# A hybrid encoder block with mixture of experts: bias products in two halves, SSD state products and output moved, router in column groups

## The reference

```
xn = rmsnorm(h); proj = xn @ w_in                  # q,k,v,r, z, xbc, dt, gates
o  = gla_scan(forward) + gla_scan(backward)        # gated linear attention, 4 heads
xbc = silu(dwconv(xbc)); xs, bm, cm = split(xbc)
y  = ssd_scan(forward) + ssd_scan(backward) + ssd_d * xs   # 4 groups of 8 heads of 64
y  = rmsnorm_per_group(y * silu(z))
mix = sigmoid(g_gla) * (o @ w_up_gla) + sigmoid(g_ssd) * (y @ w_up_ssd)
h  = h + mix @ w_out
logits = rmsnorm(h) @ w_router + b_router          # 32 experts, the best 4 per token
for each expert: hdn = x @ w1 + b1; act = gate * sigmoid(1.702 * gate) * (lin + 1); y = act @ w2 + b2
h  = h + sum(gates * y);  out = rmsnorm(h)
```

## Time and profile before

| | |
|---|---|
| runs | 2020.31, 2022.59, 2026.1 us, median 2022.59 us |
| the profiled execution | 2024.75 us |
| its span | 2023.0 us, 26649 instructions |
| busy share of the span | PE 97%, PEld 79%, DVE 77%, ACT 60%, POOL 12% |
| granted TensorE clock, mean | 0.987 |
| DMA | 540.21 MB, mean 267 GB/s |

### The profile page before, as it was taken

How to read it: one execution, slowest core, us unless ns; L and a number is a source line. 1 busy time by engine, 2 the same in 40 slices (tenths; PEclk the granted TensorE clock), 3 DMA queues, 4 the chain that set the end, 5 groups by cost and what they waited for, 6 DMA issues and landing times.

```text
span 2023.0 us, 26649 instructions
## 1 busy us (share of the span) xinstructions
PE 1969.2 (97%) x9610; PEld 1597.8 (79%) x9610; DVE 1555.2 (77%) x1499; ACT 1219.2 (60%) x1064; POOL 246.9 (12%) x175
## 2 busy tenths in 40 slices
PE   8999999999999999999999999999999999999998
PEld 6787777777768788778888888888888888888886
DVE  6655447878864335579889898998989899898987
ACT  6545444635434223357777777777777777777775
POOL 0000204263421000101010100001000001101000
PEclk9999999999999999789999999999999999999999
DMA  5233444354426934489999999999999999999995
GB/s 148 53 96 88 148 118 137 94 175 153 130 64 238 295 100 161 148 303 385 373 372 381 368 379 367 375 377 366 383 366 375 369 375 378 366 377 372 370 361 195
DMA packets 211720, 540.21 MB, mean 267 GB/s; under 512 B 16339, under 2 KB 131445, under 8 KB 174728
## 3 DMA queue, kind: packets, MB, share of 16 engines
q1 hardware_dynamic: 204368, 518.46, 70.2%
q0 software_dynamic: 7056, 20.80, 4.5%
q10 hardware_dynamic: 232, 0.08, 0.0%
HBM read 512.08 MB, written 31.20 MB: 269 GB/s over the span
## 4 chain that ended last, share of the span: by engine, by line
PE 65%; DMA 3%; issue 2%; DVE 1%; SPq 1%; ACT 1%; POOL 0%; DVEq 0%; POOLq 0%; ACTq 0%
PE ps L1847 32%; PE ps L1907 16%; PE ps L244 3%; PE ps L245 3%; PE ps L246 3%; DMA residual_rows<-late_b 2%; PE ps L1840 1%; PE ps L1815 1%; PE ps L1880 1%; SPq L2276 1%; DMA ssd_low<-ssd_out_T 1%; PE ps L1636 1%; PE ps L2010 1%; PE ps L1556 1%; DVE w_low L1745 0%
## 5 line engine op out<-in xcount | busy, mean ns | idle before, releaser
L1745 DVE TENSOR_TENSOR w_low<-ring_b,w_high 128x2048 fp32r<-128x2048 f32 x192 | 437.5, 2288 | 51.1 <-ACT w_high L1739 49.1
L1745 DVE TENSOR_TENSOR w_low<-ring_a,w_high 128x2048 fp32r<-128x2048 f32 x192 | 437.1, 2287 | 49.8 <-ACT w_high L1739 47.8
L1739 ACT ACTIVATE w_high<-ring_a 128x2048 fp32r<-128x2048 f32 x192 | 368.4, 1920 | 153.8 <-PE ps L1847 117.1
L1739 ACT ACTIVATE w_high<-ring_b 128x2048 fp32r<-128x2048 f32 x192 | 368.7, 1921 | 145.6 <-PE ps L1847 108.9
L1847 PE MATMUL ps<-w_high,rows_high 128*128 128x512 f32 x1024 | 403.4, 394 | 0.6 <-DVE w_low L1745 0.4
L1847 PE MATMUL ps<-w_high,rows_low 128*128 128x512 f32 x1024 | 400.3, 391 | 0.0
L1847 PE MATMUL ps<-w_low,rows_high 128*128 128x512 f32 x1024 | 399.7, 390 | 0.0
L1847 PEld LDWEIGHTS ps<-w_high,rows_high 128*128 128x128 f32 x1024 | 193.1, 189 | 42.7 <-DVE w_low L1745 3.0
L1847 PEld LDWEIGHTS ps<-w_high,rows_low 128*128 128x128 f32 x1024 | 192.8, 188 | 41.2
L1847 PEld LDWEIGHTS ps<-w_low,rows_high 128*128 128x128 f32 x1024 | 193.0, 189 | 39.9
L239 DVE TENSOR_TENSOR unit_low<-unit_raw,unit_high 128x1024 fp32r<-128x1024 f32 x108 | 142.6, 1330 | 98.5 <-ACT unit_high L234 98.4
(11 more groups left out here) (381 smaller groups left out, 2882.7 us busy)
## 6 DMA issues: line engine op xcount, KB each, us to landing
ring_a<-in_w SPq DMA_DIRECT2D x192, 1024.0 KB, 7.7
ring_b<-in_w SPq DMA_DIRECT2D x192, 1024.0 KB, 7.5
unit_raw<-in_w_in SPq DMA_DIRECT2D x80, 512.0 KB, 4.0
temps<-cum_rows SPq DMA_DIRECT2D x16, 1024.0 KB, 8.3
unit_raw<-in_w_up_ssd SPq DMA_DIRECT2D x16, 512.0 KB, 7.9
ssd_out_T<-y_high SPq DMA_DIRECT2D x4, 1024.0 KB, 6.3
ssd_out_T<-y_low SPq DMA_DIRECT2D x4, 1024.0 KB, 6.5
ssd_high<-ssd_out_T SPq DMA_DIRECT2D x4, 1024.0 KB, 11.4
```

The lines of the kernel that those rows point to most:

```text
L1739: nc.scalar.activation(w_hi[:, split_at(it, j)], slot(at, 1)[:, 0, :], ACT.Copy).then_inc(w_hi_ok, 1)
L1745: nc.vector.tensor_tensor(w_lo[:, split_at(it, j)], slot(at, 1)[:, 0, :], w_hi[:, split_at(it, j)].bitcast(F32), ALU.subtract).then_inc(w_ ...
```

## The change

- `ssd_pe`: the two state products of step 0 come after tile 1's products inside the chunk, ahead of the fifth piece, where they came after tile 3's. In `ssd_dve`, `to_end(0)`, which feeds them, comes ahead of `masked(0)`, where it came after the split of the fifth piece.
- `ssd_act`: the third piece's copy and the first two `keep_x` come ahead of `silu(4)`.
- The last group's output isn't stored and loaded: the mix reads `y_hi` and `y_lo` where they are. They get the place that `ssd_high3` had, and `in_w` moves behind `x_e`.
- The router: each matmul with 128 stationary columns becomes four with 32, each in its column group.
- The bias: `b1_s` is half as wide; partitions 0 to 63 hold the gate half (high, low), 64 to 127 the linear half plus one. Each of the four matmuls reads one half of the partitions. b1 comes in four loads; the cleared rows and the row of ones go.
- The end adjusts a semaphore's count (`r_in_at`), since group 3's is no longer raised by loads.

```diff
@@ SSD, TensorE
+            def states_pe(s):
+                for d in range(2):
+                    t = step_tiles(s)[d]
+                    pe.wait_ge(xe_ok, g * 6 + 2 * s + d + 1)
+                    if s == 0 and g:
+                        pe.wait_ge(ss_ok, g * 6)
+                    nc.tensor.matmul(ps[:, 6 + d, :], b_n[:, t, :], (x_e if s else in_w)[d], start=True, stop=True).then_inc(su_ps, 1)
...
                 last.then_inc(yi_ps, 1)
+                if t == 1:
+                    states_pe(0)
                 if 0 < t < 3:
                     piece(pe, n0 + 3 + t)
...
-                    if s < NT - 1:
-                        pe.wait_ge(xe_ok, g * 6 + 2 * s + d + 1)
...
+                if 0 < s < NT - 1:
+                    states_pe(s)
                 piece(pe, n0 + 6 + s)
@@ SSD, ScalarE
             silu(3)
+            piece_take(act, n0 + 2)
+            keep_x(0)
+            keep_x(1)
             silu(4)
-            piece_take(act, n0 + 2)
-            for i in range(4):
-                keep_x(i)
+            keep_x(2)
+            keep_x(3)
             silu(5)
@@ SSD, VectorE
             v.wait_ge(cb_ps, g + 1)
+            to_end(0)
             masked(0)
...
             split_low(v, n0 + 4)
-            to_end(0)
             y_begin(0)
@@ last group's output
-                store_y(sp, g)
+                if g < GR - 1:
+                    store_y(sp, g)
...
-            sp.wait_ge(y_out, 32 * GR)
+            sp.wait_ge(y_out, 32 * (GR - 1))
+            sp.wait_ge(y_lo_ok, GR * 4)
...
-            load_y(3)
@@ router
-                last = nc.tensor.matmul(ps[:, 2 * t, 0:NE], f_T[:, k, tokens(t)], wr_w[:, k, :], start=k == 0, stop=k == NK - 1)
+                for u in range(4):
+                    rows = slice(u * 32, (u + 1) * 32)
+                    last = nc.tensor.matmul(ps[rows, 2 * t, 0:NE], f_T[:, k, t * P + u * 32:t * P + (u + 1) * 32], wr_w[:, k, :],
+                                            start=k == 0, stop=k == NK - 1, tile_position=(0, u * 32))
@@ bias
-            for n in range(4):
-                nc.tensor.matmul(ps[:, n, :], pick[:, :], b1_s[:, n * 512:(n + 1) * 512], start=True, stop=False)
+            for n in range(2):
+                for half in range(2):
+                    rows = slice(half * 2 * NE, (half + 1) * 2 * NE)
+                    nc.tensor.matmul(ps[:, 2 * half + n, :], pick[rows, :], b1_s[rows, n * 512:(n + 1) * 512], start=True, stop=False)
...
-            for half in range(2):
-                sp.dma_start(b1_rows[half * NE:(half + 1) * NE, :], b1).then_inc(b1_in, 16)
+            for part in range(4):
+                cols = slice(part // 2 * DFF, (part // 2 + 1) * DFF)
+                sp.dma_start(b1_rows[part * NE:(part + 1) * NE, :], b1[:, cols]).then_inc(b1_in, 16)
...
                     nc.scalar.activation(b1_s[0:2 * NE, :], b1_rows[0:2 * NE, :], ACT.Copy).then_inc(b1_hi, 1)
+                    nc.scalar.activation(b1_s[2 * NE:P, :], b1_rows[2 * NE:P, :], ACT.Identity, bias=1.0).then_inc(b1_hi, 1)
...
-            nc.vector.memset(b1_s[2 * NE:P, :].bitcast(F32), 0.0).then_inc(one_zero, 1)
...
+                    nc.vector.scalar_tensor_tensor(b1_s[linear_low, :], b1_rows[linear_low, :], 1.0, b1_s[linear_low, :].bitcast(F32),
+                                                   ALU.add, ALU.subtract).then_inc(b1_lo, 1)
...
-            nc.vector.tensor_tensor(expert_at, ident[:, 0:NE], ident[:, NE:2 * NE], ALU.add).then_inc(one_zero, 1)
-            v.wait_ge(one_zero, 2)
-            nc.vector.memset(expert_at[2 * NE:2 * NE + 1, :], 1.0).then_inc(b1_lo, 1)
+            nc.vector.tensor_reduce(expert_at, ident[:].rearrange("p (k e) -> p e k", e=NE), AX.X, ALU.add).then_inc(b1_lo, 1)
```

More of the change, by code:

```diff
@@ L1038, in build @@
         s_st = [take(GW) for _ in range(2)]
-        in_w = [take(GW) for _ in range(2)]
         cb_d = take(SEQ).rearrange("p (t i) -> p t i", t=NT)
@@ L1045, in build @@
         z_odd = take(NT * GW).rearrange("p (t n) -> p t n", t=NT)
+        used[0] = AT_Y - AT_T + (GR - 1) * 2 * NT * GW
         y_hi = at("y_high", AT_T + used[0], NT * GW, F32R)
@@ L1053, in build @@
         x_D = x_e
+        in_w = [take(GW) for _ in range(2)]
         def by_head(ap):
@@ L1123, in ssd_pe @@
                         nc.tensor.matmul(ps[:, 2 + d, :], xcT[:, 5, tokens(t)], s_st[d], start=True, stop=True).then_inc(in_ps, 1)
-                    if s < NT - 1:
-                        pe.wait_ge(xe_ok, g * 6 + 2 * s + d + 1)
-                        if s == 0 and g:
-                            pe.wait_ge(ss_ok, g * 6)
-                        nc.tensor.matmul(ps[:, 6 + d, :], b_n[:, t, :], (x_e if s else in_w)[d], start=True, stop=True).then_inc(su_ps, 1)
+                if 0 < s < NT - 1:
+                    states_pe(s)
                 piece(pe, n0 + 6 + s)
@@ L1494, in build @@
         oT_hi, oT_lo = (at(n, AT_XN + i * NK * SEQ, NK * SEQ, F32R) for i, n in enumerate(("gla_high", "gla_low")))
-        yT_s = [[at(f"ssd_{n}{g}", AT_Y + g * 4096 + i * 2048, 4 * SEQ, F32R) for i, n in enumerate(("high", "low"))] for g in range(GR)]
+        yT_s = [[at(f"ssd_{n}{g}", AT_Y + g * 4096 + i * 2048, 4 * SEQ, F32R) for i, n in enumerate(("high", "low"))] for g in range(GR - 1)] + [[y_hi, y_lo]]
         mixT_hi, mixT_lo = (at(n, AT_MIX + i * NK * SEQ, NK * SEQ, F32R) for i, n in enumerate(("mix_high", "mix_low")))
@@ L1508, in build @@
         ring = [at(n, o, RING // 2 * UNIT) for n, o in (("ring_a", AT_GATES), ("ring_b", AT_RAW))]
-        b2_w, b1_rows = misc[:, 0:D], late_c[:, D:D + 2 * DFF]
+        b2_w, b1_rows = misc[:, 0:D], late_c[:, D:D + DFF]
         def slot(s, k):
@@ L1565, in build @@
         b1_lo = sem("b1_lo")
-        one_zero = sem("one_zero")
         slot_ok = sem("slot_ok")
@@ L1580, in build @@
         a_hi, a_lo = (small_r(n, NK * WIDE) for n in ("act_high", "act_low"))
-        b1_s = small_r("bias_split", 2 * DFF)
+        b1_s = small_r("bias_split", DFF)
         pick = small_r("pick", WIDE)
@@ L1981, in build @@
         r_in = y_in
+        r_in_at = (48, 48, 48, 16)
         sT_ps, sT_ps0 = small_ps, 1
@@ L2088, in residual @@
             def residual(t):
-                pe.wait_ge(r_in[t], 48)
+                pe.wait_ge(r_in[t], r_in_at[t])
                 for j in range(2):
@@ L2140, in finish_dve @@
                     v.wait_ge(fin_ps, fin_ps0 + t + 1)
-                    v.wait_ge(r_in[t], 48)
+                    v.wait_ge(r_in[t], r_in_at[t])
                     row = fin[:, t, :].rearrange("p (a b) -> p a b", a=2)
@@ L2330, in mix_tensor @@
                         if c == 0 and k % 4 == 0:
-                            pe.wait_ge(y_in[q // 4], 32)
+                            if q // 4 < GR - 1:
+                                pe.wait_ge(y_in[q // 4], 32)
+                            else:
+                                pe.wait_ge(y_lo_ok, GR * 4)
                         y = tuple(chunk(a, q % 4) for a in yT_s[q // 4])
@@ L2485, in mix_vector @@
                 if t == 1:
[L2486 to L2488 removed]
+                    v.wait_ge(b1_hi, 2)
+                    gate_low, linear_low = slice(NE, 2 * NE), slice(3 * NE, 4 * NE)
+                    nc.vector.tensor_tensor(b1_s[gate_low, :], b1_rows[gate_low, :], b1_s[gate_low, :].bitcast(F32),
                                             ALU.subtract).then_inc(b1_lo, 1)
+                    nc.vector.scalar_tensor_tensor(b1_s[linear_low, :], b1_rows[linear_low, :], 1.0, b1_s[linear_low, :].bitcast(F32),
+                                                   ALU.add, ALU.subtract).then_inc(b1_lo, 1)
             def pick_rows(t):
```

7 lines of the change are left out of this document (1 added, 6 removed).

## The result

| | before | after |
|---|---|---|
| median of five runs | 2020.31 us (2019.21 to 2026.10) | 2009.46 us (2007.44 to 2010.57) |
| ratio of the times | | 0.994, 95% interval 0.9923 to 0.9957 |
| the profiled execution | 2024.75 us | 2009.46 us |
| its span, mean granted clock | 2023.0 us, 0.987 | 2007.7 us, 0.989 |
| instructions | 26649 | 27027 |

What follows compares the result with a forecast made beforehand. TensorE's own instructions were taken to bound the expert loop, DMA loaded but not binding. Gains of 5.4 + 6.3 + 1.9 + 2.0 = 15.6 us, from the median 2022.59, gave 2007 us, range 2000 to 2015.

Steps and rivals of the forecast that it cites:

- case (e): Whole kernel: the edits do what the prediction says, range 2003 to 2011 us; chance 57%.
- Bias halves: Expert loop: half-height bias block takes 0.84 us instead of 1.01, gaining 0.17 us a pass, 5.4 us in all.
- Pairing: Bias block: half-height products on different row groups run side by side, so four cost 2 x 0.23 us plus 0.38.
- Passes 35.27 us apart: Expert loop, sign in the profile after: passes 35.27 us apart, where they were 35.44.
- the sign of being wrong: Expert loop: the prediction is wrong if passes are still 35.4 us or more apart.
- moves along: Expert loop: VectorE, with 3.5 us to spare a pass, keeps up because its split of the next weights waits for TensorE.
- Rival (c): Bias block: the drain is hidden behind the transposes ahead, gaining 17.6 instead of 5.4 us, 1994.8 us; chance 8%.
- State products ahead of the fifth piece: SSD: state products fill TensorE's wait, gaining 4.2 us in groups 0 to 2 and 2.1 in group 3.
- The push on VectorE: SSD groups 0 to 2: scaled copies ahead of the masks delay VectorE's later steps and the fifth piece by 0.32 us.
- Just in time: SSD, first states: they end at 426.67, with the shift 427.0, and TensorE comes to them at 427.1.
- Last output on chip: Mix: keeping the last group's output on chip removes TensorE's 1.78 us wait and slow restart, gaining 1.9 us.
- Router: Router: column groups make its products cheaper until VectorE's token choice is late; 2.0 us gained, between -1.2 and +3.2.

## Why the prediction was right, and where not

The time, 2009.46 us, lies in the likeliest case (e), 2003 to 2011. That the sum of 15.6 us matches the profiles' 15.3 is luck in part, since 3.4 us of the latter are the clock's. Term by term:

- **Bias halves, 5.4 us: over-sized.** It brought 3.2 us, and 3.1 when undone alone. Pairing, the step that could have failed, holds: 0.67 us for four. The mis-sized terms are the ends of the block. I took 0.38 us from the f32 block of line 965, entry 0.09 behind a 512-column product. Behind the 96-column transposes the entry shows as 0.15 us, the block takes 0.21 us more than its two pairs (0.67 - 2 x 0.23), and the first weight product 0.10 more: 0.46 us in place of 0.38. From the transposes' start to the second weight product it is 1.75 us against 1.84: 0.09 us a pass, 2.9 us in 32 passes, where I had 0.17. "Passes 35.27 us apart" was 35.35, close under the 35.4 that I had named as the sign of being wrong.
- **What the Trainium skill says of it** (TensorEngine Tiling (Array Packing), sections Theoretical Speedup and Key Properties): the first gives up to twice the rate for a contraction of 64 or less, the second says that a change of tiling mode drains TensorE. Both hold here, on different numbers. A pair alone goes at twice the rate (0.23 us in the kernel with the bias twice); entering and leaving the block takes most of it back in a block of only four.
- **VectorE "moves along": right with less room than I gave it.** 3.5 us to spare said nothing about a wait inside its order. Without the bias the loop meets that wait and needs 35.27 us a pass on average, only 0.12 us under the present average. Rival (c), 17.6 us, could not have come for this reason alone: it needs passes of 34.89 us.
- **State products ahead of the fifth piece, 4.2 + 2.1: right, a little small.** Groups 0 to 2 gained 4.9 us, group 3's part 2.0. The push on VectorE was forecast at 0.32 us; counted from each group's first transposes the fifth piece starts at 14.69 us instead of 14.56, 0.13 later. "Just in time" for the next states held: they end at 425.04, TensorE comes at 425.58. Undone alone the move costs 7.1 us, or about 5.6 without the clock's early fall in that profile. ScalarE's new order, which I expected to free 2.93 us of waiting and cap at VectorE's chain, is worth 0.5 us.
- **Last output on chip, 1.9 us: right.** 2.15 between the profiles, 2.5 undone alone.
- **Router, 2.0 us: the mechanism fails.** A record costs 0.011 us, not the 0.03 of the earlier trace rows, so TensorE gained more than I took, and the next thing late was VectorE, as I said. But VectorE was already next with the old router when the clock stayed up. I read a price at 0.50 clock as a property of the kernel, when it was one of that execution. The estimate that I made from the Trainium skill's page TensorEngine Tiling (Array Packing), section Instruction Overhead (60 cycles for each record, one after the other, 3.2 us) fails as well: 1.36 us for 128 records. That speaks against counting the records in a row, not against the page's minimum: with four groups side by side each has 32 records in 1.36 us, 0.042 us each.

Without the router the stages sum to 3.2 + 6.9 + 2.2 = 12.3 us. The ratio of the runs, 0.994, is 12.1 us, with an interval of 8.7 to 15.6, and the medians differ by 10.9; the runs alone don't exclude the 15.3 us of the profiles, but those contain one execution of before whose clock fell early. My forecast took 15.6 us off a median of 2022.59, where the wider set of runs has 2020.31. So the base was 2.3 us too high and the gain 3.3 us (by stages) to 4.7 us (by medians) too large, and the two errors partly cancel: that 2007 came within 2.5 us of the time is luck in part. Inside the gain the bias (too much) and SSD (too little) partly cancel; the router's 2.0 us stays.

What stays open is why the clock fell early there. From the windows it fell some 17.7 us after the first router transposes (68% of 835 to 840 at the lower level), and 23 us after them with the old router in the kernel after (72% of 830 to 835). In all thirteen profiles of the later kernels it fell 20.8 to 24.1 us after them. The work of TensorE in the stretch doesn't explain the difference: in both kernels the first router products start 13.54 us after the first transposes and the last transposes 17.03 us after them. It seems to be one of the execution, not of the kernel before. In the profile of before the lower level lasts 30.7 us around the router, and no profile here has less than 19 us of it elsewhere; both together would make the mean clock of a run at most 0.988, by estimate, and 12 of the 18 later runs of before have 0.989 or more. But of before there is one profile, so this isn't shown directly. In an execution that has the early fall the column groups would save about the 3.4 us; no run shows one, so that is an argument and not shown.

## What to carry to other kernels

Two half-height products in two row groups cost one full product, in both orders tried, but a block of them costs about 0.4 us beyond its pairs (0.82 us net for two pairs of 0.23): make the block long or leave it. Before a duration at half clock enters a sum, ask whether the clock is the kernel's or the execution's, by reading what would end the stretch at full clock. And a loop's next bound is found by taking away more than the edit does: leaving the bias out altogether showed a wait for a landing DMA that holds the loop only 0.12 us a pass below where it is, and that no busy share shows. And before a stage's difference between two profiles is put down to an edit, read the granted clock in that stage in both: here it made up nearly all of one stage's gain and a fifth of one experiment's.

## What was not expected of the hardware

- Products on one half of the rows aren't held up by earlier ones in the list on the other half: 0.67 us in alternation, 0.66 with two of one half ahead of two of the other.
- f32 records with 32 moving columns: 0.11 us with 128 stationary columns, 0.032 with 64 in two groups, 0.011 with 32 in four.
- The same 32 records at the same place: 3.66 us in one profile, 6.88 in another, with TensorE fully busy ahead of both.
- A change of shape costs 0.09 us behind a 512-column product and 0.15 us behind 96-column transposes; moved ahead of the transposes most of it comes back behind the block (0.66 for 0.60 us in them, 0.31 for 0.23 in the product after them).
